# First conv chunk on unnormalised x: the tiles of chunk 0 take x times gain, and the row factor comes at their eviction

## The chip, the cores and the metric

The kernel runs on one core of a Trainium2 chip. The metric is the device time of one execution in microseconds; the engines named here are TensorE (PE, matmuls into the eight PSUM banks `ps`), VectorE (DVE), ScalarE (ACT), GpSimd (POOL, idle here) and SyncE (SP, which only issues transfers).

## What is computed

A block of 512 tokens of width 1024 in float32: a conv layer and an attention layer, each with a gated side input, and behind them a second block with its own attention, a recurrent branch and two feed-forward layers. The change lies in the first matmuls of the first layer:

```python
h = rms_norm(x, norm_g[0])              # x * rsqrt(mean(x*x) + EPS) * g, row by row (a row is a token)
u = h @ w_in
a, b, gate = jnp.split(u, [CONV_DIM, 2 * CONV_DIM], axis=-1)
y = a * jax.nn.sigmoid(b)
y = lax.conv_general_dilated(y, dw[:, None, :], window_strides=(1,), padding=((CONV_WIDTH - 1, 0),), ...,
                             feature_group_count=CONV_DIM) + dw_b      # 31 taps, each channel by itself
y = layer_norm(y, ln_g, ln_b)
y = jax.nn.silu(y) * jax.nn.silu(gate)
x = x + y @ w_out
```

The row factor rsqrt(mean(x*x) + EPS) is one number per token, so a matmul of x times gain can be multiplied by it afterwards.

## The kernel before

All activations lie with the channels on the 128 partitions and the 512 tokens along the free side; x is `X`, eight blocks of 128x512, loaded in four quarters of two blocks (128x1024). A matmul of full precision is made of three: each operand is cut into a high part (rounded to the matmul's input form) and a low part (the rest), and high times high, high times low and low times high are added in PSUM. So a weight tile of 128x1024 is first loaded into `w_raw` by SyncE, then ScalarE copies it to `w_hi`, and VectorE subtracts to `w_lo`; in the code of either engine this is `prep()`. There are four slots (`RING`): a load waits until the w_lo of the tile four before is done, and a w_hi until TensorE is through with it. TensorE's `tile()` is eight blocks of 128x128, three matmuls each, 24 in all.

Each engine has a program of its own, carried out in the order in which it is written, and they meet only at semaphores. Stage 0 is the conv layer's input, in eight chunks c of 128 channels. A chunk has four weight tiles: a, b, gate (all three on `H_hi`, `H_lo`, the normalised x), and a diagonal tile with eight of the 31 taps, on `cv_yh`, `cv_yl`, the halves of y = a * sigmoid(b). The other 23 taps are VectorE's (`cv_acc`), and its last addition gives `cv_Y` (`y_done`). TensorE adds up the columns of `cv_Y` of chunk c - 1 between the gate tile and the diagonal tile of chunk c, so it waits there for `y_done`, and then for `y_lo` of its own chunk. The tiles are numbered through: chunk 0 has tiles 0 to 3, chunk 1 has 4 to 7.

Ahead of chunk 0 stand the squares of x (ScalarE, `sq` and `tmp`), their sums by a matmul with ones into bank 7 (TensorE, `sq_used`), the guess of the row factor (`guess`, ScalarE, exp of -0.5 log), its Newton step (`newton`, VectorE, into `rx`), and `normed`: per block VectorE multiplies x, gain and factor into `tmp`, ScalarE copies it to `H_hi` and VectorE subtracts to `H_lo`. After these come two weight tiles' halves and `pl_hi`, `pl_lo`, the halves of the side input (`pl_raw`, 128x2048).

The transfers at the start: ScalarE's queue has parameters (128x364), constants (128x640) and the four quarters of x, SyncE's has four weight tiles, two loads of the side input and the late parameters, and then one weight tile after another.

## Time and profile before

| | |
|---|---|
| median of three runs | 2136.47 us (2135.02 to 2147.24) |
| the profiled execution | 2154.28 us |
| its span | 2152.5 us |
| TensorE busy in it | 2004.0 us (93%) |
| VectorE busy in it | 1237.8 us (58%) |
| ScalarE busy in it | 849.3 us (39%) |
| granted TensorE clock, mean over the span | 0.955 |

Times in the rows further down are microseconds from the span's start. Busy shares are means over stages of different kinds; for a change at the start, the rows of the start count.

### The profile page before, as it was taken

What the parts mean: (1) busy time and instruction counts of PE and PEld (TensorE: products, weight loads), DVE (VectorE), ACT (ScalarE), POOL (GpSimd) and SP (SyncE); (2) the same over time, 40 slices, a digit from 0 to 9 for tenths busy, and PEclk for the clock granted to TensorE, in tenths of its full rate; (3) what the DMA queues carried; (4) which work ended last, traced back from release to release, by engine and by line L of the source; (5) the groups of instructions that cost most, each with busy time, mean ns of one, the idle gap of its engine ahead of it and who ended that gap; (6) DMA issues with size and microseconds to landing.
All of it is one profiled execution on the core that took longest, in us unless ns stands there. A gap on an engine that the chain in (4) does not pass through costs nothing.

```text
span 2152.5 us, 23084 instructions
## 1 busy us (share of the span) xinstructions
PE 2004.0 (93%) x8460; PEld 1544.5 (72%) x8460; DVE 1237.8 (58%) x1859; ACT 849.3 (39%) x1156; POOL 0.2 (0%) x4
## 2 busy tenths in 40 slices
PE   6999788899999997899999989998898899999999
PEld 4888466677777676688888866666665578888887
DVE  5999666765766636644443355578654365444422
ACT  4333534344444334443432244444342334434311
POOL 0000000000000000000000000000000000000000
PEclk9999899899999879999999989989998999999999
DMA  4323222322212111233333412111211132332332
GB/s 169 100 78 100 91 69 69 103 74 64 63 53 64 42 49 59 77 99 97 91 103 114 132 59 89 49 39 49 69 59 39 46 110 90 97 97 93 103 116 89
DMA packets 49136, 175.17 MB, mean 81 GB/s; under 512 B 6048, under 2 KB 6176, under 8 KB 48288
## 3 DMA queue, kind: packets, MB, share of 16 engines
q1 hardware_dynamic: 44496, 159.67, 24.1%
q10 hardware_dynamic: 4560, 14.41, 2.0%
q8 instruction: 53, 0.87, 0.2%
q14 instruction: 27, 0.22, 0.0%
HBM read 166.19 MB, written 6.29 MB: 80 GB/s over the span
## 4 chain that ended last, share of the span: by engine, by line
PE 49%; DVE 8%; ACT 3%; issue 1%; DVEq 0%; ACTq 0%
PE ps L1471 45%; PE ps L1860 1%; DVE w_lo L904 1%; PE ps L1873 1%; DVE tmp L1325 1%; PE ps L1889 1%; ACT w_hi L418 1%; PE ps L1780 1%; DVE ds_acc L1245 1%; DVE ds_mx L1244 0%; DVE ds_P L1387 0%; DVE X L956 0%; DVE var L939 0%; DVE var L915 0%; DVE ds_P L1407 0%
## 5 line engine op out<-in xcount | busy, mean ns | idle before, releaser
L1471 PE MATMUL ps<-H_hi,w_hi 128*128 128x512 f32 x1600 | 658.3, 411 | 43.7 <-DVE H_lo L963 14.9
L1471 PE MATMUL ps<-H_lo,w_hi 128*128 128x512 f32 x1600 | 635.0, 397 | 0.0
L1471 PE MATMUL ps<-H_hi,w_lo 128*128 128x512 f32 x1600 | 633.9, 396 | 0.0
L904 DVE TENSOR_TENSOR w_lo<-w_raw,w_hi 128x1024 fp32r<-128x1024 f32 x298 | 363.2, 1223 | 368.6 <-ACT w_hi L418 363.9
L1471 PEld LDWEIGHTS ps<-H_hi,w_hi 128*128 128x128 f32 x1600 | 307.6, 192 | 141.4 <-issue 33.4
L418 ACT ACTIVATE w_hi<-w_raw 128x1024 fp32r<-128x1024 f32 x298 | 311.5, 1048 | 145.3 <-PE ps L1471 143.8
L1471 PEld LDWEIGHTS ps<-H_lo,w_hi 128*128 128x128 f32 x1600 | 308.3, 193 | 69.9 <-issue 8.6
L1471 PEld LDWEIGHTS ps<-H_hi,w_lo 128*128 128x128 f32 x1600 | 307.4, 192 | 66.5
L1471 PE MATMUL ps<-mid_hi,w_lo 128*128 128x512 f32 x352 | 138.8, 394 | 0.0
L1471 PE MATMUL ps<-mid_lo,w_hi 128*128 128x512 f32 x352 | 138.8, 394 | 0.0
L1471 PE MATMUL ps<-mid_hi,w_hi 128*128 128x512 f32 x352 | 138.8, 394 | 0.0
L1065 DVE SCALAR_TENSOR_TENSOR cv_acc<-cv_a,par,cv_acc 128x509 f32<-128x509 f32 (+6 forms) x168 | 111.4, 727 | 0.0
L418 ACT ACTIVATE mid_hi<-tmp 128x512 f32 x44 | 27.8, 632 | 195.4 <-DVE tmp L1029 195.4
L956 DVE SCALAR_TENSOR_TENSOR X<-ps,X 128x512 f32<-128x512 f32 (+1 forms) x36 | 27.0, 750 | 125.1 <-PE ps L1471 125.0
L466 ACT ACTIVATE r<-X 128x512 f32<-128x512 f32 x40 | 25.3, 632 | 175.6 <-DVE X L956 175.6
L1471 PE MATMUL ps<-G_hi,w_hi 128*128 128x512 f32 x128 | 54.6, 426 | 26.1 <-DVE X L956 10.5
L1471 PEld LDWEIGHTS ps<-mid_lo,w_hi 128*128 128x128 f32 x352 | 65.9, 187 | 16.3
L1471 PEld LDWEIGHTS ps<-mid_hi,w_hi 128*128 128x128 f32 x352 | 65.9, 187 | 16.2
L1471 PEld LDWEIGHTS ps<-mid_hi,w_lo 128*128 128x128 f32 x352 | 65.9, 187 | 16.1
L1025 DVE TENSOR_TENSOR tmp<-ps,rx 128x512 f32<-128x512 f32 x44 | 30.4, 691 | 68.1 <-PE ps L1471 68.1
L1496 PE MATMUL ps<-sq,con 128*128 128x512 f32 x84 | 50.0, 691 | 9.3 <-DVE rs L921 7.5
L521 ACT ACTIVATE sq<-sq 128x512 f32<-128x512 f32 x44 | 27.8, 633 | 77.2 <-DVE sq L1020 77.2
(295 smaller groups left out, 2421.0 us busy)
## 6 DMA issues: line engine op xcount, KB each, us to landing
w_raw<-weights SPq DMA_DIRECT2D x298, 512.0 KB, 3.6
X<-x ACTq DMA_DIRECT2D x4, 512.0 KB, 11.2
pl_P<-spill ACTq DMA_DIRECT2D x1, 2048.0 KB, 8.3
spill<-X ACTq DMA_DIRECT2D x8, 256.0 KB, 2.0
X<-spill ACTq DMA_DIRECT2D x2, 1024.0 KB, 5.1
out<-X SPq DMA_DIRECT2D x8, 256.0 KB, 5.1
at_mask<-masks ACTq DMA_DIRECT2D x1, 1536.0 KB, 6.2
at_pair<-at_raw ACTq DMA_DIRECT2D x96, 16.0 KB
```

Of the source, the lines that this page charges most:

```text
L418: return act.activation(out_ap, in_ap, ACT.Copy)
L466: act.activation(out_t, X[:, m:m + n, :], ACT.Square).then_inc(x_squared, 1)
L521: act.activation(sq[:, j, :], sq[:, j, :], ACT.Silu).then_inc(gated, 1)
L904: dve.tensor_tensor(w_lo[:, s, :], w_raw[:, s, :], w_hi[:, s, :].bitcast(F32), ALU.subtract)\
L956: dve.scalar_tensor_tensor(X[:, m:m + n, :], src, scale, X[:, m:m + n, :], ALU.mult, ALU.add)\
L1025: dve.tensor_tensor(tmp[:, j, :], ps[:, bank_of(k.n["prep"] - AHEAD - 1), :], rx[:, :], ALU.mult).then_inc(read_out, 1)
L1065: instr = dve.scalar_tensor_tensor(acc, a[:, 0:S - t], w, acc, ALU.mult, ALU.add)
L1245: link(dve.match_replace(acc, ds_mx[:, :], acc, TAKEN))
L1325: link(dve.reciprocal(tmp[:, 0, :], tmp[:, 0, :]))
L1471: mm = pe.matmul(ps[:, bank, :], w, x, start=first and n == 0 and q == 0, stop=last and n == len(blocks) - 1 and q == 2)
L1496: pe.matmul(ps[:, bank, :], ones if lhsT is None else lhsT, sq[:, (k.n[sq_done] - 1) % 2, :], start=c == 0, stop=c == n - 1).then_inc(sq_u ...
L1780: pe.matmul(ps[:, 6 + h % 2, 0:P * (b + 1)], ds_U[rows, 4 + h // 2, b * P:(b + 1) * P], ds_kvi[rows, 1, 0:P * (b + 1)], start=True, stop=T ...
```

## The change

The first conv chunk's three tiles run on `G_hi`, `G_lo`, the halves of x times gain without the row factor. ScalarE makes `G_hi` as each quarter lands, ahead of its square; VectorE makes `G_lo`. TensorE sums the squares inside tile 0, ahead of blocks 1, 3, 5 and 7. VectorE multiplies chunk 0's three results by the row factor `rx` when it takes them out of PSUM (`first_conv`, `first_gate`), and these evictions stand inside `normed`, behind its blocks 2 and 5. The other seven chunks still take `H_hi`, `H_lo`. SyncE's third transfer and all behind it wait for the second quarter of x. The weight tiles' halves move with it: the third tile's stand ahead of the guess, the fourth's in `first_conv`, the fifth's and sixth's in `first_gate`, and in chunk 0's taps there are two in place of four.

```diff
--- before.py
+++ after.py
@@ -22,6 +22,7 @@
 D = 1024
 KC = D // P
 RING = 4
+FIRST_CONV, FIRST_GATE = 2, 5
 AHEAD = 2
 EPS = 1e-6
 NEG = -1e30
@@ -374,6 +375,8 @@
         @block.sync
         def _(sp):
             for u in range(RING):
+                if u == 2:
+                    sp.wait_ge(x_loaded[1], 16)
                 sp.dma_start(w_raw[:, u, :], weights[u]).then_inc(landed[u], 16)
             for q in range(2):
                 sp.dma_start(pl_raw[:, 2 * q:2 * q + 2, :], ple_in[q]).then_inc(ple_loaded, 16)
@@ -532,26 +535,46 @@
                 act.dma_start(X[:, 2 * q:2 * q + 2, :], x_in[:, 2 * q:2 * q + 2, :]).then_inc(x_loaded[q], 16)
             begin(k, 0)
             prep()
+            act.wait_ge(par_loaded, 16)
             for q in range(4):
                 act.wait_ge(x_loaded[q], 16)
+                for m in (2 * q, 2 * q + 1):
+                    act.activation(G_hi[:, m, :], X[:, m, :], ACT.Copy, scale=col("norm_g0", m)).then_inc(split_hi, 1)
+                    k.up(split_hi)
                 if q >= 2:
                     act.wait_ge(sq_used, q - 1)
                 act.activation((sq, tmp)[q % 2][:, :, :], X[:, 2 * q:2 * q + 2, :], ACT.Square).then_inc(sq_done, 1)
                 k.up(sq_done)
                 if q == 1:
                     prep()
+            prep()
             logs()
-            act.wait_ge(par_loaded, 16)
             guess(7, 1.0 / D, sq_used, 4)
             for c in range(KC):
                 split(H_hi[:, c, :], c % 2)
-            prep()
-            prep()
+                if c == FIRST_CONV:
+                    act.wait_ge(scaled, k.up(scaled))
+                    act.activation(cv_sg[:, 0, :], cv_sg[:, 0, :], ACT.Sigmoid).then_inc(gated, 1)
+                    k.up(gated)
+                    act.wait_ge(read_out, k.up(read_out))
+                    copy(cv_yh[:, 0, PAD:PAD + S], cv_a[:, 0, :]).then_inc(y_hi, 1)
+                    k.up(y_hi)
+                    prep()
+                if c == FIRST_GATE:
+                    act.wait_ge(scaled, k.up(scaled))
+                    act.activation(cv_G[:, 0, :], cv_G[:, 0, :], ACT.Silu).then_inc(gate_out, 1)
+                    k.up(gate_out)
+                    prep()
+                    prep()
             act.wait_ge(ple_loaded, 32)
             copy(pl_hi[:, :, :], pl_raw[:, :, :]).then_inc(act_out, 1)
             k.up(act_out)
             k.up(dve_out)
-            for c in range(KC):
+            k.up(tile_done, 3 + DIAG[0])
+            prep()
+            for _ in range(DIAG[0]):
+                prep()
+            for c in range(1, KC):
                 act.wait_ge(tile_done, k.up(tile_done, 2))
                 if c >= 2:
                     act.wait_ge(read_out, k.at(read_out, -1))
@@ -963,7 +986,7 @@
                 dve.tensor_tensor(dst, src, hi.bitcast(F32), ALU.subtract).then_inc(split_lo, 1)
                 k.up(split_lo)
 
-            def normed(gain):
+            def normed(gain, between=()):
                 for c in range(KC + 1):
                     if c < KC:
                         if c >= 2:
@@ -973,6 +996,8 @@
                         k.up(tmp_done)
                     if c:
                         split(H_lo[:, c - 1, :], tmp[:, (c - 1) % 2, :], H_hi[:, c - 1, :])
+                    if c in between:
+                        between[c]()
 
             def ple(pl_P, hi, lo, gain):
                 prep()
@@ -1040,19 +1065,48 @@
             prep()
             prep()
             dve.wait_ge(par_loaded, 16)
+            for m in range(KC):
+                dve.wait_ge(split_hi, k.up(split_hi))
+                dve.scalar_tensor_tensor(G_lo[:, m, :], X[:, m, :], col("norm_g0", m), G_hi[:, m, :].bitcast(F32),
+                                         ALU.mult, ALU.subtract).then_inc(split_lo, 1)
+                k.up(split_lo)
+            prep()
             newton(7, 1.0 / D, rx, sq_used, 4)
-            normed("norm_g0")
-            prep()
-            prep()
+
+            def first_conv():
+
+                dve.wait_ge(tile_done, 2)
+                dve.tensor_tensor(cv_sg[:, 0, :], ps[:, 1, :], rx[:, :], ALU.mult).then_inc(scaled, 1)
+                k.up(scaled)
+                link(dve.tensor_tensor(cv_a[:, 0, :], ps[:, 0, :], rx[:, :], ALU.mult))
+                dve.wait_ge(gated, k.up(gated))
+                dve.tensor_tensor(cv_a[:, 0, :], cv_a[:, 0, :], cv_sg[:, 0, :], ALU.mult).then_inc(read_out, 1)
+                dve.wait_ge(read_out, k.up(read_out))
+                dve.wait_ge(y_hi, k.up(y_hi))
+                dve.tensor_tensor(cv_yl[:, 0, PAD:PAD + S], cv_a[:, 0, :], cv_yh[:, 0, PAD:PAD + S].bitcast(F32),
+                                  ALU.subtract).then_inc(y_lo, 1)
+                k.up(y_lo)
+                prep()
+
+            def first_gate():
+
+                dve.wait_ge(tile_done, 3)
+                dve.tensor_tensor(cv_G[:, 0, :], ps[:, 4, :], rx[:, :], ALU.mult).then_inc(scaled, 1)
+                k.up(scaled)
+                prep()
+                prep()
+
+            normed("norm_g0", between={FIRST_CONV + 1: first_conv, FIRST_GATE + 1: first_gate})
             dve.wait_ge(act_out, k.up(act_out))
             dve.tensor_tensor(pl_lo[:, :, :], pl_raw[:, :, :], pl_hi[:, :, :].bitcast(F32), ALU.subtract)\
                 .then_inc(dve_out, 1)
             k.up(dve_out)
             for c in range(KC):
-                dve.wait_ge(gated, k.up(gated))
                 a = cv_a[:, c % 2, :]
-                dve.tensor_tensor(a, ps[:, 2 * (c % 2), :], cv_sg[:, c % 2, :], ALU.mult).then_inc(read_out, 1)
-                dve.wait_ge(read_out, k.up(read_out))
+                if c:
+                    dve.wait_ge(gated, k.up(gated))
+                    dve.tensor_tensor(a, ps[:, 2 * (c % 2), :], cv_sg[:, c % 2, :], ALU.mult).then_inc(read_out, 1)
+                    dve.wait_ge(read_out, k.up(read_out))
                 for n, t in enumerate(DVE_TAPS[c]):
                     w = col("taps", 32 * c + CONV_W - 1 - t)
                     acc = cv_acc[:, n % 2, t:S]
@@ -1065,13 +1119,13 @@
                         instr = dve.scalar_tensor_tensor(acc, a[:, 0:S - t], w, acc, ALU.mult, ALU.add)
                     instr.then_inc(dve_chain, 1)
                     k.up(dve_chain)
-                    if n == 2:
+                    if n == 2 and c:
                         dve.wait_ge(y_hi, k.up(y_hi))
                         dve.tensor_tensor(cv_yl[:, c % 2, PAD:PAD + S], a, cv_yh[:, c % 2, PAD:PAD + S].bitcast(F32),
                                           ALU.subtract).then_inc(y_lo, 1)
                         k.up(y_lo)
                         prep()
-                    elif n in (5, 9, 13) or n == 14 and DIAG[c] == 2:
+                    elif n in ((5, 9, 13) if c else (9, 13)) or n == 14 and DIAG[c] == 2:
                         prep()
                 dve.wait_ge(dve_chain, k.at(dve_chain))
                 link(dve.tensor_tensor(cv_acc[:, 0, 1:S], cv_acc[:, 0, 1:S], cv_acc[:, 1, 1:S], ALU.add))
@@ -1454,7 +1508,7 @@
             k = Counts()
             k.up(x_summed)
 
-            def tile(groups, arriving=None, room=None):
+            def tile(groups, arriving=None, room=None, between=()):
 
                 s = k.n.get("tile", 0) % RING
                 k.up("tile")
@@ -1465,6 +1519,8 @@
                     for n, (b, x_hi, x_lo) in enumerate(blocks):
                         if arriving is not None:
                             pe.wait_ge(split_lo, arriving[n])
+                        if n in between:
+                            between[n](n // 2)
                         wh = w_hi[:, s, b * P:(b + 1) * P]
                         wl = w_lo[:, s, b * P:(b + 1) * P]
                         for q, (w, x) in enumerate(((wh, x_hi), (wh, x_lo), (wl, x_hi))):
@@ -1541,12 +1597,15 @@
 
             begin(k, 0)
             pe.wait_ge(con_loaded, 16)
-            for q in range(4):
+            def sums(q):
+
                 pe.wait_ge(sq_done, k.up(sq_done))
                 for j in range(2):
-                    mm = pe.matmul(ps[:, 7, :], ones, (sq, tmp)[q % 2][:, j, :], start=q + j == 0, stop=q + j == 4)
+                    mm = pe.matmul(ps[:, 7, :], ones, (sq, tmp)[q % 2][:, j, :], start=q + j == 0, stop=q + j == 4,
+                                   skip_group_check=True)
                 mm.then_inc(sq_used, 1)
                 k.up(sq_used)
+
             k.up(r0_done)
             k.up(rs_done)
             k.up(split_lo, KC)
@@ -1555,11 +1614,15 @@
                 if c >= 2:
                     pe.wait_ge(read_out, k.at(read_out, -1))
                 a = 2 * (c % 2)
-                tile([(a, True, True, blocks(H_hi, H_lo))], None if c else arrivals())
-                tile([(a + 1, True, True, blocks(H_hi, H_lo))])
+                if c == 1:
+                    k.up(split_lo, KC)
+                hi, lo = (H_hi, H_lo) if c else (G_hi, G_lo)
+                tile([(a, True, True, blocks(hi, lo))], arrivals() if c < 2 else None,
+                     between=() if c else {2 * q + 1: sums for q in range(4)})
+                tile([(a + 1, True, True, blocks(hi, lo))])
                 if c:
                     pe.wait_ge(gate_out, c)
-                tile([(4, True, True, blocks(H_hi, H_lo))])
+                tile([(4, True, True, blocks(hi, lo))])
                 if c:
                     pe.wait_ge(y_done, c)
                     pe.matmul(ps[:, 6, :], ones, cv_Y[:, c - 1, :], start=c == 1, stop=False, skip_group_check=True)
```

The two programs at three places, each engine's own order, with what an instruction waits for in brackets.

VectorE from its first weight halves on, before:

```order
L904 TENSOR_TENSOR w_lo<-w_raw,w_hi 128x1024 [waits hi_done] x2
L915 TENSOR_SCALAR var<-ps 128x512 [waits r0_done,par_loaded]
L919 TENSOR_TENSOR rx<-r 128x512 [waits dve_chain]
L920 SCALAR_TENSOR_TENSOR rx<-rx,var 128x512 [waits dve_chain]
L921 SCALAR_TENSOR_TENSOR rx<-rx,r 128x512 [waits dve_chain]
```

and now:

```order
L927 TENSOR_TENSOR w_lo<-w_raw,w_hi 128x1024 [waits hi_done] x2
L1070 SCALAR_TENSOR_TENSOR G_lo<-X,par,G_hi 128x512 [waits split_hi,par_loaded]
L1070 SCALAR_TENSOR_TENSOR G_lo<-X,par,G_hi 128x512 [waits split_hi] x7
L927 TENSOR_TENSOR w_lo<-w_raw,w_hi 128x1024 [waits hi_done]
L938 TENSOR_SCALAR var<-ps 128x512 [waits r0_done]
```

Eight G_lo have come between the second weight tile's low part and the Newton step, and the third tile's low part as well.

ScalarE from its first weight half to the guess, before (`r` is the guess's buffer):

```order
L418 ACTIVATE w_hi<-w_raw 128x1024 [waits landed0]
L539 ACTIVATE sq<-X 128x1024 [waits x_loaded0]
L539 ACTIVATE tmp<-X 128x1024 [waits x_loaded1]
L418 ACTIVATE w_hi<-w_raw 128x1024 [waits landed1]
L539 ACTIVATE sq<-X 128x1024 [waits sq_used,x_loaded2]
L539 ACTIVATE tmp<-X 128x1024 [waits sq_used,x_loaded3]
L441 ACT_TABLE_LOAD
L449 ACTIVATE r<-ps,par 128x512 [waits sq_used,par_loaded]
```

and now, up to the third square:

```order
L421 ACTIVATE w_hi<-w_raw 128x1024 [waits landed0]
L542 ACTIVATE G_hi<-X,par 128x512 [waits x_loaded0,par_loaded]
L542 ACTIVATE G_hi<-X,par 128x512
L546 ACTIVATE sq<-X 128x1024
L542 ACTIVATE G_hi<-X,par 128x512 [waits x_loaded1]
L542 ACTIVATE G_hi<-X,par 128x512
L546 ACTIVATE tmp<-X 128x1024
L421 ACTIVATE w_hi<-w_raw 128x1024 [waits landed1]
L542 ACTIVATE G_hi<-X,par 128x512 [waits x_loaded2]
L542 ACTIVATE G_hi<-X,par 128x512
L546 ACTIVATE sq<-X 128x1024 [waits sq_used]
```

The second weight tile's high part still stands behind the second square, which now has four G_hi ahead of it.

VectorE in the middle of the normalisation, where the first evictions are, now (before, the six rows with tmp and H_lo follow each other, and the product cv_a<-ps,cv_sg comes after all eight H_lo, two w_lo and pl_lo):

```order
L986 TENSOR_TENSOR H_lo<-tmp,H_hi 128x512 [waits split_hi]
L1079 TENSOR_TENSOR cv_sg<-ps,rx 128x512 [waits tile_done]
L1081 TENSOR_TENSOR cv_a<-ps,rx 128x512
L1083 TENSOR_TENSOR cv_a<-cv_a,cv_sg 128x512 [waits gated,dve_chain]
L1086 TENSOR_TENSOR cv_yl<-cv_a,cv_yh 128x512 [waits y_hi,read_out]
L927 TENSOR_TENSOR w_lo<-w_raw,w_hi 128x1024 [waits hi_done]
L994 SCALAR_TENSOR_TENSOR tmp<-X,par,rx 128x512 [waits split_lo]
L986 TENSOR_TENSOR H_lo<-tmp,H_hi 128x512 [waits split_hi]
```

Chunk 0's y and its halves have moved ahead of five of the eight H blocks; its taps stay behind pl_lo.

## Rows read from the trace of the kernel before

**Rows 1.** The page, busy time of each engine (share of the span) and its instructions

```profile
PE 2004.0 (93%) x8460; PEld 1544.5 (72%) x8460; DVE 1237.8 (58%) x1859; ACT 849.3 (39%) x1156; POOL 0.2 (0%) x4
```

**Rows 2.** Timeline of ScalarE, first 40 us: start, duration, instruction, idle before it

```profile
10.02 1.06 ACT L539 ACTIVATE sq<-X 128x1024 f32<-128x1024 f32 x1 [3.50 <-DMA X<-x]
12.58 1.06 ACT L539 ACTIVATE tmp<-X 128x1024 f32<-128x1024 f32 x1 [1.50 <-DMA X<-x]
13.54 1.04 ACT L418 ACTIVATE w_hi<-w_raw 128x1024 fp32r<-128x1024 f32 x1
...
21.14 0.69 ACT L449 ACTIVATE r<-ps,par 128x512 f32<-128x512 f32 x1 [1.08 <-PE ps L1547]
...
37.85 1.90 ACT L418 ACTIVATE pl_hi<-pl_raw 128x2048 fp32r<-128x2048 f32 x1
```

**Rows 3.** Timeline of TensorE: the sums, and where tiles 0, 1, 3, 4 and chunk 2 start

```profile
11.22 3.75 PE L1547 MATMUL ps<-sq,con 128*128 128x512 f32 x4 [11.22 <-ACT sq L539]
...
17.45 1.88 PE L1547 MATMUL ps<-sq,con 128*128 128x512 f32 x4
19.17 1.88 PE L1547 MATMUL ps<-tmp,con 128*128 128x512 f32 x4
27.80 0.77 PE L1471 MATMUL ps<-H_hi,w_hi 128*128 128x512 f32 x1 [6.75 <-DVE H_lo L963]
...
37.63 0.39 PE L1471 MATMUL ps<-H_hi,w_hi 128*128 128x512 f32 x1
...
48.52 0.40 PE L1471 MATMUL ps<-cv_yh,w_hi 128*128 128x512 f32 x1
...
54.11 0.39 PE L1471 MATMUL ps<-H_hi,w_hi 128*128 128x512 f32 x1
...
76.90 0.39 PE L1471 MATMUL ps<-H_hi,w_hi 128*128 128x512 f32 x1
```

**Rows 4.** Timeline of VectorE, up to chunk 2

```profile
14.62 1.23 DVE L904 TENSOR_TENSOR w_lo<-w_raw,w_hi 128x1024 fp32r<-128x1024 f32 x1 [6.83 <-ACT w_hi L418]
...
30.46 0.75 DVE L971 SCALAR_TENSOR_TENSOR tmp<-X,par,rx 128x512 f32<-128x512 f32 x1
...
39.78 2.29 DVE L1048 TENSOR_TENSOR pl_lo<-pl_raw,pl_hi 128x2048 fp32r<-128x2048 f32 x1 [0.39 <-ACT pl_hi L418]
...
44.64 0.55 DVE L1060 TENSOR_SCALAR cv_acc<-cv_a,par 128x512 f32<-128x512 f32 x1
...
65.00 0.69 DVE L1079 TENSOR_TENSOR cv_Y<-cv_acc,ps 128x512 f32<-128x512 f32 x1
65.84 0.69 DVE L1054 TENSOR_TENSOR cv_a<-ps,cv_sg 128x512 f32<-128x512 f32 x1 [0.16 <-ACT cv_sg L558]
...
68.09 0.68 DVE L1070 TENSOR_TENSOR cv_yl<-cv_a,cv_yh 128x512 fp32r<-128x512 f32 x1
...
88.66 0.69 DVE L1054 TENSOR_TENSOR cv_a<-ps,cv_sg 128x512 f32<-128x512 f32 x1 [1.05 <-ACT cv_sg L558]
```

**Rows 5.** Windows: from:to, length, each engine's busy time, granted clock, DMA share, GB/s

```profile
0.00:8.00 8.00, 0.00 (x0) 0.00 (x0) 1.41 (x3) 2.34 (x2) 0.20 (x4) 1.00 0.77 280
4.00:10.00 6.00, 0.00 (x0) 0.00 (x0) 1.23 (x1) 2.34 (x2) 0.00 (x0) 1.00 1.03 413
27.80:33.30 5.50, 5.50 (x12) 3.33 (x13) 5.36 (x9) 2.52 (x4) 0.00 (x0) 0.50 0.00 0
219.50:224.50 5.00, 0.02 (x1) 0.00 (x0) 4.90 (x8) 0.00 (x0) 0.00 (x0) 0.70 0.16 65
...
228.00:231.50 3.50, 3.45 (x4) 1.46 (x5) 3.50 (x6) 1.22 (x2) 0.00 (x0) 0.50 0.00 0
```

**Rows 6.** Timeline of ScalarE, two scaled copies and a weight half in a row

```profile
803.43 1.32 ACT L476 ACTIVATE G_hi<-X,par 128x512 fp32r<-128x512 f32 x2
804.66 1.04 ACT L418 ACTIVATE w_hi<-w_raw 128x1024 fp32r<-128x1024 f32 x1
```

## Prediction

> **What bounds the kernel now.** The page's busy line comes first: TensorE has work for 93% of the span, VectorE for 58% [rows 1]. Such an average hides the part that the diff touches, the first 77 us, so the timelines of the engines over that stretch come next. ScalarE squares each quarter of x when it lands, the first at 10.02 us and the second at 12.58, and takes the guess of the row factor once the sums of squares are there, at 21.14 [rows 2]. TensorE sums the squares from 11.22 to 21.05, is then idle for 6.75 us, runs the first tile from 27.80 to 37.63, and from there has tile after tile: tile 1 starts at 37.63, tile 3 at 48.52, tile 4 at 54.11, and the third chunk (chunk 2) begins at 76.90 [rows 3]. That last number is the yardstick of this forecast. From 76.90 to the end of the conv stage TensorE never stops: a chunk is four tiles and a column sum, VectorE has some 1 us to spare in each (its c=2 product waits 1.05 us for the sigmoid [rows 4]), and the product of chunk 1 has started at 65.84, 7 us before TensorE could use it. What the change makes of the time is what it makes of 76.90; everything behind it is moved with it.
>
> **TensorE alone gains.** The first conv chunk's three tiles now take x times gain, split (G_hi, G_lo), and the sums of squares are done between their blocks. So nothing on TensorE waits for the row factor until the diagonal tile. Its work is the same: 24 matmuls a tile and eight sums.
>
> **When x is there.** SyncE now holds its third and fourth weight tile, both ple loads and the late parameters until the second quarter of x has landed. Before, the transfers together moved 280 GB/s over the first 8 us, 2.24 MB, and 413 from 4 us on [rows 5]. Up to the first quarter there are now two weight tiles (0.52 MB each, 128x1024 of four bytes), parameters and constants (0.51, from 128x364 and 128x640) and the quarter itself (0.52), 2.08 MB, which is reached at 7.7 us; the second quarter follows 0.52 MB later, at 8.9. The two ends are 7.5 and, if nothing is won, the 10.0 of before. What speaks for 7.7 is the spacing of the quarters before [rows 2]: 2.56 us for 0.52 MB is 205 GB/s, half of what was moved. The Trainium skill says the same (DMA: Bandwidth & Descriptors, Issuing engines are not separate DMA queues): transfers of all issuing engines run on the same 16 DMA engines and interleave. By that rule the quarters come 1.3 us apart and the sum below holds; without it, it would be 2.3 us more.
>
> **What holds TensorE's start.** ScalarE does per quarter two scaled copies (1.23 us from start to the next start) and a square (0.96) [rows 2, 6]: 2.19 us. Two quarters from 7.7 end at 12.1, then comes the split of the second weight tile, to 13.15. VectorE's order is the point: its second w_lo stands ahead of all eight G_lo. It already waited 6.83 us for ScalarE's w_hi there, and everything behind it with it [rows 4]. So its second w_lo runs from 13.2 to 14.45, G_lo of block 0 to 15.2, and TensorE starts at 15.25, though x and the first G_hi were there at 8.4. The Trainium skill (TensorE: Matmul & The Clock Gate, Architectural detail) calls the queues of ScalarE and VectorE strictly first in, first out; by it this block stands in full, and without it the sum would be that of the second rival below.
>
> **When the sums are ready.** At 2.4 GHz a tile's 24 matmuls take 5.45 us (two of them 37.63 to 48.52), so a block of three 0.68, and two sums 1.72 (17.45 to 19.17); at 1.2 GHz I take 1.28 for a block and 3.4 for two sums, near twice that, as the first two of before bear out (3.75 with their end) [rows 3]. The clock rose after some 5.7 us of work both times that it starts from rest here (from 27.80 it was 0.50 up to 33.3 at least, and the second pair of sums, between 11.22 and 17.45, is the last that is slow) [rows 3, 5]. From 15.25: block 0 to 16.5, first sums to 19.95, block 1 to 21.1 with the clock rising at about 20.95, block 2 to 21.8, sums 23.5, two blocks 24.9, sums 26.6, two blocks 28.0, last sums 29.85. ScalarE keeps ahead of that (its third square may start at 19.95, its fourth at 23.5). Before, the sums ended at 21.05. **The row factor comes 8.8 us later**, since the 24 matmuls are now in its way and start late. TensorE itself ends the first tile at 30.4 and the third at 41.3, 7.2 us before the 48.52 of before.
>
> **VectorE's chain, from 29.85.** Guess, Newton steps and the first three H splits follow as before (VectorE is through with the third block at 30.46) [rows 4], all 8.8 later: 39.25. Then comes what is new. Two evictions with the row factor and the product, 0.73 each (a VectorE pass over 128x512 is 0.69 [rows 4], 0.04 for the wait on it): 41.45. ScalarE's sigmoid (0.6) lies under the second of them. The copy to cv_yh with its hand-over 0.75, the split 0.7: 42.9. The fourth weight tile's halves follow one after the other and end at 44.4, where the diagonal tile can start: TensorE has waited 3.15 us. Three pairs of a product and a split, 1.39 each (two passes, as eight before): 48.6. Eviction of the gate: 49.3; ScalarE's silu to 50.0, then its weight split, then VectorE's: 52.25, where tile 4 starts (TensorE free at 50.05: 2.2 of idle). The next w_lo to 53.4, the last H splits to 55.5. Now VectorE waits for pl_hi, which ScalarE can only begin after the last H_hi: 54.8 plus 1.90, and pl_lo takes 2.29: 59.05 [rows 2, 4]. Then the taps of chunk 0: from 44.64 to 65.69 it was 21.05 us [rows 4]; a split (0.68) and two w_lo (1.23 each) have gone elsewhere, less the 0.1 that each lies over the next: 18.2. **Chunk 0's y ends at 77.25, where it ended at 65.69.** Within it the w_lo for the gate tile of chunk 1, now behind ten taps (0.66 each after two shorter ones, 6.1), ends at 66.35; TensorE, free at 63.15, waits 3.2 and is through at 71.8.
>
> **The place where it is paid.** TensorE waits for that y before the column sum (y_done), 5.5 us, and then for y_lo of chunk 1, which takes 2.93 after the product may start (65.84 to 68.77 [rows 4]): 80.2. The diagonal tile (5.59, as 48.52 to 54.11) ends at 85.85, against 76.90: **+8.95 us**. From there TensorE is the bound again: VectorE is up to 1.8 us late in chunk 2 and regains 1 a chunk.
>
> **The clock after the 5.5 us.** Before, after an idle stretch of 5.00 us that ended at 224.5 the granted clock was 0.50 until 231.5, 7 us past the restart, and after 6.75 us idle it stayed low for some 6 more [rows 3, 5]. With the restart at 77.3 the diagonal tile from 80.25 runs at 1.2 GHz up to 83.3 or 84.3 and loses 1.5 to 2.0 us; I take 1.8. The ends are 0, if the clock holds, and 5.6, if it is low for the whole tile. The earlier waits (3.15, 2.2, 3.2) may cost clock too, but VectorE is what is waited for up to 77.3 and covers it. The extra work that nobody waits for (SyncE's held loads: the third weight tile lands near 13, is split by ScalarE at about 25 and needed at 35.9; ple near 17, needed at 54.8) I put at nothing: their cover is 10 us and more.
>
> **Sum.** 8.95 + 1.8 = +10.8 us. The profiled execution took 2154.28 us (2152.5 of span and 1.8 around it), so one of the changed kernel should take 2165; the median of the runs is 2136.47, 17.8 lower, over the same stages, and with the same addition gives **2147.3**.
>
> **Rivals.**
> - *TensorE's gain stays.* If VectorE were in time, the 7.2 us of the third tile would be kept: 2129.3. For it: TensorE has 93% of the span, VectorE 58%, and 6.75 us before were its idle wait for the row factor. Against it: VectorE was busy without a break from 44.64 to 65.69 and has got 8 passes for G_lo, 3 evictions and several handshakes; chunk 2 at 69.7 wants the diagonal tile at 64.1 and so y of chunk 0 by 61. It is the case on the other side. 12%.
> - *G_lo isn't held behind the second w_lo.* TensorE would start at 9.2, the sums end at 23.7 (then bound by ScalarE's squares), the chain would be 6.1 shorter: 85.85 becomes 79.8, +2.9, so 2139.4. Against it: the order of VectorE's program and the 6.83 us of before. 8%.
> - *Holding the loads brings nothing.* x at 10.0: +2.3 more, 2149.6. 12%.
> - *The clock stays low through the diagonal tile*, because four waits in 36 us make it fall again and again: 8.95 + 5.6, 2151.0. 8%.
>
> **How the numbers follow.** My forecast has 60%. The single runs of before lie 12 us apart, so even its exact case can be read 2 or 3 us off. The range 2135 to 2153 takes in the forecast with its ends and all rivals but the gain. A difference of 1% is 21 us, about what a measurement of this kernel can tell from none; no case reaches it: 1% for faster, 97% within, 2% for slower (the last two rivals together and one more wait of the kind).
>
> **What would show it.** In the profile of the changed kernel: the first scaled copy starts near 7.7; VectorE's second w_lo ends at 14.4 with G_lo right behind; the last sum of squares ends near 29.9; the diagonal tile starts near 44.4 after a wait for VectorE; y of chunk 0 at 77.3; TensorE idle for over 5 us ahead of the first column sum; chunk 2 begins at 86 to 88. The prediction is wrong if TensorE starts before 12, if the sums end before 26, or if chunk 2 begins before 77.

## The result and the profile after

| | before | changed |
|---|---|---|
| median of 17 runs each | 2135.21 us | 2151.34 us |
| lowest to highest | 2133.65 to 2152.28 | 2145.09 to 2166.35 |
| ratio, with 95% interval | | 1.0055 [1.0028, 1.0081] |
| the profiled execution, its span | 2154.28, 2152.5 | 2157.8, 2155.7 |
| granted clock in it | 0.955 | 0.961 |
| chunk 2 starts | 76.90 [rows 3] | 86.89 |
| last y of the conv stage ends | 224.47 | 234.43 |

The changed kernel is slower by 0.55% by the ratio, which is 11.7 us of 2135.21, with an interval of 6 to 17 us; the two medians lie 16.1 us apart. The forecast was 10.8 us. The yardstick of the forecast, the start of chunk 2, has moved by 9.99 us, and 150 us later the shift is still 9.96: nothing is won back within the conv stage.

The page's busy line of the changed kernel is nearly that of [rows 1], and tells nothing of this:

```profile
PE 1996.6 (93%) x8460; PEld 1539.1 (71%) x8460; DVE 1244.2 (58%) x1870; ACT 854.3 (40%) x1164; POOL 0.2 (0%) x4
```

ScalarE's timeline of the changed kernel, against [rows 2]:

```profile
8.56 1.33 ACT L542 ACTIVATE G_hi<-X,par 128x512 fp32r<-128x512 f32 x2 [2.27 <-DMA X<-x]
9.79 1.04 ACT L546 ACTIVATE sq<-X 128x1024 f32<-128x1024 f32 x1
...
20.25 1.06 ACT L546 ACTIVATE sq<-X 128x1024 f32<-128x1024 f32 x1 [5.07 <-PE ps L1604]
...
29.59 0.69 ACT L452 ACTIVATE r<-ps,par 128x512 f32<-128x512 f32 x1 [2.92 <-PE ps L1604]
```

The first quarter of x is there 1.46 us sooner than before, and the third square now waits 5.07 us for TensorE, whose sums stand inside the first tile. The guess, 21.14 before, comes at 29.59. VectorE's timeline, against [rows 4]:

```profile
13.98 1.22 DVE L927 TENSOR_TENSOR w_lo<-w_raw,w_hi 128x1024 fp32r<-128x1024 f32 x1 [6.44 <-ACT w_hi L421]
15.12 4.06 DVE L1070 SCALAR_TENSOR_TENSOR G_lo<-X,par,G_hi 128x512 fp32r<-128x512 f32 x6
...
38.72 0.68 DVE L1079 TENSOR_TENSOR cv_sg<-ps,rx 128x512 f32<-128x512 f32 x1
...
55.54 2.29 DVE L1101 TENSOR_TENSOR pl_lo<-pl_raw,pl_hi 128x2048 fp32r<-128x2048 f32 x1 [1.11 <-ACT pl_hi L421]
...
75.23 0.69 DVE L1133 TENSOR_TENSOR cv_Y<-cv_acc,ps 128x512 f32<-128x512 f32 x1
...
78.07 0.68 DVE L1124 TENSOR_TENSOR cv_yl<-cv_a,cv_yh 128x512 fp32r<-128x512 f32 x1
```

Six G_lo start in one piece right behind the second w_lo, ahead of which VectorE stood idle for 6.44 us: their inputs had become ready one after the other since 9. The chain from the guess on then ends at 75.92, where it ended at 65.69. TensorE's timeline, against [rows 3]:

```profile
16.02 0.76 PE L1527 MATMUL ps<-G_hi,w_hi 128*128 128x512 f32 x1 [16.02 <-DVE G_lo L1070]
...
17.43 2.78 PE L1604 MATMUL ps<-sq,con 128*128 128x512 f32 x4
...
21.45 1.88 PE L1604 MATMUL ps<-tmp,con 128*128 128x512 f32 x4
...
27.67 1.88 PE L1604 MATMUL ps<-tmp,con 128*128 128x512 f32 x4
...
43.87 0.47 PE L1527 MATMUL ps<-cv_yh,w_hi 128*128 128x512 f32 x1 [2.42 <-DVE w_lo L927]
...
51.30 0.50 PE L1527 MATMUL ps<-H_hi,w_hi 128*128 128x512 f32 x1 [1.59 <-DVE w_lo L927]
...
65.19 0.47 PE L1527 MATMUL ps<-H_hi,w_hi 128*128 128x512 f32 x1 [2.74 <-DVE w_lo L927]
...
75.97 2.07 PE L1628 MATMUL ps<-cv_Y,con 128*128 128x512 f32 x2 [5.09 <-DVE cv_Y L1133]
...
78.80 0.80 PE L1527 MATMUL ps<-cv_yh,w_hi 128*128 128x512 f32 x1 [0.76 <-DVE cv_yl L1124]
...
86.89 0.39 PE L1527 MATMUL ps<-H_hi,w_hi 128*128 128x512 f32 x1
```

The one idle stretch of 6.75 us ahead of tile 0 has become five later ones, all for VectorE: 2.42, 1.59, 2.74, 5.09 and 0.76 us. The fourth is the one that decides: the column sum waits 5.09 us for chunk 0's y. Windows over that place, with the columns of [rows 5] (the five busy times are of TensorE, its weight loads, VectorE, ScalarE and GpSimd):

```profile
65.00:70.00 5.00, 4.81 (x21) 4.05 (x22) 5.00 (x9) 0.00 (x0) 0.00 (x0) 1.00 0.34 111
70.00:75.00 5.00, 0.88 (x4) 0.38 (x3) 4.97 (x9) 0.00 (x0) 0.00 (x0) 0.89 0.29 98
75.00:80.00 5.00, 3.27 (x5) 1.50 (x6) 4.93 (x9) 3.43 (x5) 0.00 (x0) 0.50 0.00 0
80.00:85.00 5.00, 5.00 (x15) 3.89 (x14) 5.00 (x8) 0.98 (x2) 0.00 (x0) 0.59 0.49 144
```

VectorE is busy for all but 0.1 us from 65 to 85, TensorE works 0.88 us of the five from 70, and the granted clock falls with it and is back only in the course of the fourth window: the diagonal tile takes 8.09 us (78.80 to 86.89), where chunk 0's took 5.59 in [rows 3] and chunk 1's own 5.99 in the kernel before (70.91 to 76.90).

### The profile page after: what moved, and what is told of

Read it like the earlier page. It is cut to its first block, busy times and chain, and to the rows that moved or that the text cites. A ratio compares the mean times of both kernels' runs of the same rounds, so it can differ in the third digit from the quotient of the medians.

```text
span 2155.7 us, 23107 instructions
## 1 busy us (share of the span) xinstructions
PE 1996.6 (93%) x8460; PEld 1539.1 (71%) x8460; DVE 1244.2 (58%) x1870; ACT 854.3 (40%) x1164; POOL 0.2 (0%) x4
## 4 chain that ended last, share of the span: by engine, by line
PE 49%; DVE 9%; ACT 3%; issue 1%; DVEq 0%; ACTq 0%
PE ps L1527 44%; PE ps L1923 1%; DVE w_lo L927 1%; PE ps L1936 1%; PE ps L1952 1%; DVE tmp L1379 1%; DVE ds_acc L1299 1%; PE ps L1843 1%; ACT w_hi L421 1%; DVE ds_mx L1298 1%; DVE ds_P L1441 0%; DVE X L979 0%; DVE var L962 0%; DVE var L938 0%; DVE rs L944 0%
## 5 line engine op out<-in xcount | busy, mean ns | idle before, releaser
L1527 PE MATMUL ps<-H_hi,w_hi 128*128 128x512 f32 x1576 | 642.5, 408 | 40.7 <-DVE H_lo L974 11.7
L1527 PE MATMUL ps<-H_lo,w_hi 128*128 128x512 f32 x1576 | 621.0, 394 | 0.0
L1527 PE MATMUL ps<-H_hi,w_lo 128*128 128x512 f32 x1576 | 620.2, 394 | 0.0
L1527 PEld LDWEIGHTS ps<-H_hi,w_hi 128*128 128x128 f32 x1576 | 300.3, 191 | 133.8 <-issue 28.0
L1527 PEld LDWEIGHTS ps<-H_lo,w_hi 128*128 128x128 f32 x1576 | 300.7, 191 | 68.1 <-issue 8.3
L1527 PEld LDWEIGHTS ps<-H_hi,w_lo 128*128 128x128 f32 x1576 | 300.1, 190 | 64.5
L1527 PE MATMUL ps<-G_hi,w_hi 128*128 128x512 f32 x152 | 65.6, 432 | 41.4 <-DVE G_lo L1070 16.0
L1527 PEld LDWEIGHTS ps<-G_hi,w_hi 128*128 128x128 f32 x152 | 29.4, 193 | 54.8 <-issue 34.0
L1527 PE MATMUL ps<-G_lo,w_hi 128*128 128x512 f32 x152 | 61.6, 405 | 0.0
```

The source lines that it names most:

```text
L1527: mm = pe.matmul(ps[:, bank, :], w, x, start=first and n == 0 and q == 0, stop=last and n == len(blocks) - 1 and q == 2)
```

## Experiments

All starts and ends below are in us from the span's start. None of the eight kernels leaves anything out. Early_half, sums_ahead, filler and before_hold ran beside each other on one chip (before: median 2136.7 of 31 runs), the other four on another (before: 2140.8 of 32); the ratio of the changed kernel is that of the section above. Repeats of one kernel spread over 12 to 26 us, so the question of what a step costs is answered by one profile of each kernel, at the start of chunk 2, and the ratio tells whether the whole time follows. Of the ratios, those of the changed kernel, no_hold, filler and early_half lie clear of 1 above it and second_bank's below it; no two of the changed kernel's variants up to pl_early can be told apart by them.

| | last sums end | y of chunk 0 ends | from the one to the other | chunk 2 starts | last y ends | ratio to before |
|---|---|---|---|---|---|---|
| before | 21.05 | 65.69 | 44.64 | 76.90 | 224.47 | 1 |
| changed | 29.55 | 75.92 | 46.37 | 86.89 | 234.43 | 1.0055 [1.0028, 1.0081] |
| before_hold | 19.96 | 64.62 | 44.66 | 75.84 | 223.41 | 0.9984 [0.9948, 1.0020] |
| no_hold | 31.39 | 77.77 | 46.38 | 88.66 | 236.23 | 1.0063 [1.0032, 1.0095] |
| early_half | 24.49 | 70.86 | 46.37 | 82.08 | 229.62 | 1.0039 [1.0002, 1.0075] |
| filler | 31.00 | 77.38 | 46.38 | 85.96 | 233.53 | 1.0066 [1.0028, 1.0104] |
| sums_ahead | 20.78 | 69.24 | 48.46 | 80.33 | 227.86 | 1.0024 [0.9990, 1.0058] |
| pl_early | 30.79 | 73.76 | 42.97 | 83.81 | 231.38 | 1.0024 [0.9995, 1.0053] |
| reordered | 21.04 | 64.48 | 43.44 | 74.97 | 222.51 | 1.0001 [0.9971, 1.0032] |
| second_bank | 20.99 | 65.62 | 44.63 | 68.54 | 222.23 | 0.9949 [0.9917, 0.9981] |

The fourth column is the table's point: in four kernels whose sums end between 24.49 and 31.39 it is the same within 0.01 us. As long as VectorE's order behind the sums is kept and TensorE is in time, whatever moves the sums moves y by as much. Where the sums come at 20.78 (sums_ahead), TensorE isn't in time any more.

### The weight half that holds VectorE (early_half)

The theory is that ScalarE's second weight half, late behind two quarters' work, holds VectorE's whole queue. It goes ahead of x, and nothing else changes:

```diff
             prep()
+            prep()
             act.wait_ge(par_loaded, 16)
             for q in range(4):
                 act.wait_ge(x_loaded[q], 16)
...
-                if q == 1:
-                    prep()
```

> The changed kernel with one step moved: ScalarE makes the second weight tile's high part right after the first, ahead of x, so that VectorE's second w_lo no longer stands in front of G_lo. Theory A (VectorE's chain behind the row factor sets chunk 2, and the blocked G_lo is a part of its lateness): TensorE starts near 10.1 us in place of 16.02, the last sums end near 24.7 in place of 29.6, and chunk 2 begins 4.9 us earlier than the changed kernel's 86.89, at 82.0, so still 5 us behind the 76.90 of before. Rival B (the block costs nothing, since TensorE's three tiles have room): chunk 2 stays at 86.9. The whole time should follow by as much, under what the repeats differ by.

VectorE and TensorE of that kernel:

```profile
8.19 1.23 DVE L926 TENSOR_TENSOR w_lo<-w_raw,w_hi 128x1024 fp32r<-128x1024 f32 x1 [0.70 <-ACT w_hi L421]
9.50 0.75 DVE L1069 SCALAR_TENSOR_TENSOR G_lo<-X,par,G_hi 128x512 fp32r<-128x512 f32 x1
```

```profile
10.39 0.76 PE L1526 MATMUL ps<-G_hi,w_hi 128*128 128x512 f32 x1 [10.39 <-DVE G_lo L1069]
...
22.61 1.88 PE L1603 MATMUL ps<-tmp,con 128*128 128x512 f32 x4
...
82.08 0.39 PE L1526 MATMUL ps<-H_hi,w_hi 128*128 128x512 f32 x1
```

The wait ahead of w_lo has shrunk from 6.44 to 0.70 us, TensorE starts 5.63 us sooner, the sums end 5.06 sooner, and chunk 2 starts at 82.08, 4.81 us sooner, where 82.0 was expected. So half of what the change costs hung on the place of one ScalarE copy. The first G_hi starts at 8.56 in the changed kernel and at 8.65 here, so G_lo's input is there at about 9.3 in both; the first G_lo starts at 15.12 in the one and at 9.50 in the other. It was only its place in the queue that held it. The Trainium skill (TensorE: Matmul & The Clock Gate, Architectural detail) calls ScalarE's and VectorE's queues strictly first in, first out, and the trace agrees.

### The sums ahead of the tile (sums_ahead)

```diff
+            for q in range(4):
+                sums(q)
...
-                     between=() if c else {2 * q + 1: sums for q in range(4)})
+                     between=())
```

> The changed kernel with the sums of squares back ahead of tile 0; the tiles still take x times gain without the row factor. Theory A (the sums inside tile 0 delay the row factor, and with it VectorE's chain): the last sums end near 20.7 in place of 29.6; VectorE then waits for tile 1, so the chain gains 6.8 us, and chunk 2 begins near 80.1, 3 us behind before. Rival B (TensorE's order doesn't matter, only its total): tile 2 ends 4 us earlier or later and chunk 2 moves by under 2 us. Rival C (what costs is the added evictions on VectorE alone): chunk 2 stays within 1 us of 86.9.

TensorE:

```profile
18.90 1.88 PE L1604 MATMUL ps<-tmp,con 128*128 128x512 f32 x4
...
20.22 0.80 PE L1527 MATMUL ps<-G_hi,w_hi 128*128 128x512 f32 x1
...
80.33 0.39 PE L1527 MATMUL ps<-H_hi,w_hi 128*128 128x512 f32 x1
```

The sums end at 20.78, 8.77 us sooner than in the changed kernel, and chunk 2 starts 6.56 us sooner, at 80.33 (80.1 was expected). Most of the difference is 2.09 us in the chain, and its row shows why: VectorE is free for the first eviction at 30.04 and waits for tile 1.

```profile
32.02 0.69 DVE L1079 TENSOR_TENSOR cv_sg<-ps,rx 128x512 f32<-128x512 f32 x1 [1.98 <-PE ps L1527]
```

This is the largest single step of the loss. The steps don't add up, since this one and early_half both work through the end of the sums (6.56 and 4.81 us are more than the 9.99 of the loss together). It also shows what the reordering can do at best: TensorE is then what the chain waits for. Yet chunk 2 is still 3.43 us later than before. The early sums alone don't mend it.

### The clock after the wait (filler)

Five matmuls whose result nobody reads, into bank 7 (free by then), stand ahead of the wait for y of chunk 0:

```diff
                 tile([(4, True, True, blocks(hi, lo))])
+                if c == 1:
+                    for j in range(5):
+                        pe.matmul(ps[:, 7, :], ones, X[:, j, :], start=True, stop=True, skip_group_check=True)
                 if c:
                     pe.wait_ge(y_done, c)
```

> The changed kernel with five extra float32 matmuls (x with ones, into bank 7, read by nobody) on TensorE ahead of its wait for chunk 0's y; they take 4.3 us of the 5.1 that it idles there. Theory A (the clock falls in that idle stretch, and the diagonal tile of chunk 1 pays for it): the granted clock stays at 1.00 from 70 to 90 us, the diagonal tile takes 5.6 us in place of 8.1, and chunk 2 begins near 84.4 in place of 86.9. Rival B (the idle stretch costs nothing beyond itself): chunk 2 stays at 86.9 or comes later by what the filler overlaps.

TensorE, and two of its windows:

```profile
17.57 3.61 PE L1604 MATMUL ps<-sq,con 128*128 128x512 f32 x4
...
73.74 4.45 PE L1628 MATMUL ps<-X,con 128*128 128x512 f32 x10
...
80.27 0.50 PE L1527 MATMUL ps<-cv_yh,w_hi 128*128 128x512 f32 x1 [1.22 <-DVE cv_yl L1124]
...
85.96 0.39 PE L1527 MATMUL ps<-H_hi,w_hi 128*128 128x512 f32 x1
```

```profile
75.00:80.00 5.00, 4.05 (x10) 1.52 (x8) 4.89 (x9) 1.97 (x3) 0.00 (x0) 1.00 0.00 0
80.00:85.00 5.00, 4.73 (x20) 3.88 (x21) 5.00 (x7) 2.44 (x3) 0.00 (x0) 1.00 0.38 108
```

The granted clock stays at 1.00, where it was 0.50 and 0.59, and the diagonal tile takes 5.69 us in place of 8.09. That is 2.4 us for the clock. One profile alone would be thin evidence, since the clock had its own course in this execution (it was also low from 66.5 to 69.9, in the gate tile, so that without the five matmuls TensorE would have idled 3.5 us here and not 5.1). But the six kernels that wait 4.65 to 5.10 us at this place all run the tile behind it at the low clock for a part, in 7.16 to 8.33 us (pl_early 7.16, reordered 7.59, no_hold 8.00, changed 8.09, sums_ahead 8.20, early_half 8.33). Chunk 2 starts only 0.93 us sooner (85.96, where 84.4 was expected), since in this execution the sums came 1.45 us later: the first pair took 3.61 us and not 2.78, with the same instructions ahead of it. That part is no effect of the edit. The ratio of 1.0066 is not below the change's 1.0055, and the intervals overlap widely, so a gain in the whole time was not measured.

### The held loads (before_hold, no_hold)

The wait on SyncE alone, in the kernel before, and the change without it:

```diff
@@ before_hold, against before
+                if u == 2:
+                    sp.wait_ge(x_loaded[1], 16)
@@ no_hold, against the changed kernel
-                if u == 2:
-                    sp.wait_ge(x_loaded[1], 16)
```

> The kernel before with one line of the change: SyncE's third and later loads wait for the second quarter of x; nothing else is changed. If the hold is what brings x early and the row factor's chain is what bounds the start, the first square starts near 8.6 in place of 10.02, the sums end 2 to 2.5 us earlier than 21.05, and chunk 2 begins at 74.4 to 75 in place of 76.90: a gain of 2 us, which the timing of whole runs can't tell. Rival: the sums run at the lower clock whatever x does, and the chain gains under 1 us.

> The changed kernel without SyncE's wait for the second quarter of x: all loads are issued at once, as before. If the hold is what brings x early (the kernel before with the hold alone had its first square at 8.61 in place of 10.02), the first scaled copy starts near 10.0 in place of 8.56, VectorE's blocked G_lo moves with it, and chunk 2 begins 1.4 us later than the changed kernel's 86.89, at 88.3. Rival (the hold is hidden behind ScalarE's own work): chunk 2 stays at 86.9.

ScalarE and TensorE of before_hold, and the first G_hi of no_hold:

```profile
8.61 1.06 ACT L541 ACTIVATE sq<-X 128x1024 f32<-128x1024 f32 x1 [2.19 <-DMA X<-x]
...
13.67 1.06 ACT L541 ACTIVATE sq<-X 128x1024 f32<-128x1024 f32 x1 [1.77 <-PE ps L1549]
```

```profile
9.81 3.75 PE L1549 MATMUL ps<-sq,con 128*128 128x512 f32 x4 [9.81 <-ACT sq L541]
...
13.36 3.17 PE L1549 MATMUL ps<-tmp,con 128*128 128x512 f32 x4
...
75.84 0.39 PE L1473 MATMUL ps<-H_hi,w_hi 128*128 128x512 f32 x1
```

```profile
10.22 1.33 ACT L540 ACTIVATE G_hi<-X,par 128x512 fp32r<-128x512 f32 x2 [3.78 <-DMA X<-x]
```

The hold brings the first quarter of x from 10.02 to 8.61 in the one kernel and from 10.22 to 8.56 in the other. Without it the change is 1.77 us later at chunk 2 (1.4 was expected). In the kernel before it is worth only 1.06 of its 1.41 us. There the first sums run at about half the rate, 3.75 and 3.17 us for a pair where later pairs take 1.88, whatever the time at which x comes, and the third square waits 1.77 us for them. (The granted clock reads 1.00 over both the slow and the fast pairs there, so the rate has to be taken from the passes themselves.) The larger gain that I expected there, 1.9 to 2.5 us, was wrong, and the smaller one of the rival, under 1 us, was nearer. The Trainium skill (DMA: Bandwidth & Descriptors, Issuing engines are not separate DMA queues) says that transfers of all issuing engines run on the same 16 DMA engines and interleave; the 1.66 us by which one queue's wait advances another's transfer agree.

### The side input's halves (pl_early)

ScalarE's pl_hi goes ahead of the guess, VectorE's pl_lo ahead of the Newton step, off the chain:

```diff
@@ ScalarE, behind the third prep() (VectorE likewise, ahead of newton; the old places are empty)
+            act.wait_ge(ple_loaded, 32)
+            copy(pl_hi[:, :, :], pl_raw[:, :, :]).then_inc(act_out, 1)
```

> The changed kernel with the side input's halves (pl_hi on ScalarE, pl_lo on VectorE) moved ahead of the guess, where both engines are idle in its profile (from 26.6 to 31). Theory A (VectorE's chain from the row factor to y of chunk 0 is what TensorE waits for): the chain loses pl_lo and its wait for pl_hi, 3.3 us, y of chunk 0 ends at 72.6 in place of 75.92, TensorE's 2.7 us of idle ahead of the gate tile go, and chunk 2 begins at 83.6, or near 81.2 if the idle stretch, now 4.6 us, doesn't let the clock fall. Rival (TensorE's own order bounds it): chunk 2 stays within 1 us of 86.9.

VectorE:

```profile
28.45 2.29 DVE L1075 TENSOR_TENSOR pl_lo<-pl_raw,pl_hi 128x2048 fp32r<-128x2048 f32 x1 [0.58 <-ACT pl_hi L421]
...
73.07 0.69 DVE L1133 TENSOR_TENSOR cv_Y<-cv_acc,ps 128x512 f32<-128x512 f32 x1
```

The chain is 3.40 us shorter, which is pl_lo's 2.29 and its wait of 1.11, to the hundredth. Chunk 2 comes 3.08 us sooner, although the sums came 1.24 us later in this execution (again by the first pair, 3.62 us): 2.16 us is what the chain less that delay gives, and the rest is the diagonal tile, 7.16 us in place of 8.09. With 1.24 us added, the 83.6 that was expected would have been 84.8; it came at 83.81.

### Both reorderings, and y ahead of the taps (reordered, second_bank)

"reordered" takes the sums ahead as sums_ahead does, makes the side input's halves early but at other places than pl_early (pl_hi right behind the guess, pl_lo ahead of the first evictions), and moves ScalarE's silu of chunk 0 behind the last H_hi:

```diff
@@ ScalarE, the silu; the edits of the sums and of the side input's halves aren't shown
             for c in range(KC):
                 split(H_hi[:, c, :], c % 2)
...
                 if c == FIRST_GATE:
-                    act.wait_ge(scaled, k.up(scaled))
-                    act.activation(cv_G[:, 0, :], cv_G[:, 0, :], ACT.Silu).then_inc(gate_out, 1)
-                    k.up(gate_out)
                     prep()
                     prep()
...
+            act.wait_ge(scaled, k.up(scaled))
+            act.activation(cv_G[:, 0, :], cv_G[:, 0, :], ACT.Silu).then_inc(gate_out, 1)
+            k.up(gate_out)
```

> The changed kernel with three moves: sums of squares ahead of tile 0 (measured alone: chunk 2 at 80.33), the side input's halves early (ScalarE right behind the guess, VectorE ahead of the first evictions, where it waits for tile 1), and ScalarE's silu of chunk 0 behind the two weight halves that VectorE waits 1.65 us for. By the chain: y of chunk 0 ends at 69.24 - 3.3 - 1.6 + 0.3 = 64.6, and chunk 2 begins at 73.1 with the clock up, 75.6 with it down, 1.3 to 3.8 us ahead of the kernel before. If something else than VectorE's chain bounds it, chunk 2 stays above 78.

TensorE:

```profile
64.54 1.93 PE L1629 MATMUL ps<-cv_Y,con 128*128 128x512 f32 x2 [4.66 <-DVE cv_Y L1132]
...
74.97 0.39 PE L1526 MATMUL ps<-H_hi,w_hi 128*128 128x512 f32 x1
```

The y of chunk 0 ends at 64.48 (64.6 was expected), chunk 2 starts at 74.97 (75.6 with the clock down), 1.93 us ahead of the kernel before, and the ratio is 1.0001. So with three things in another order the change costs nothing. Whether the tiles on unnormalised x have a part in the 1.93 us isn't shown: the held loads alone gave 1.06 of it in the kernel before, and no run puts the side input's halves early there. It gains nothing worth speaking of either, since TensorE still waits 4.66 us for VectorE's taps and runs the next tile at the low clock (7.59 us).

"second_bank" attacks that wait: VectorE makes chunk 1's product and its low half within chunk 0's taps, and the diagonal tile of chunk 1 goes to bank 7, ahead of the column sum, so that TensorE has 24 matmuls to do while y is unfinished:

```diff
@@ VectorE, in the taps of chunk 0 (beside the edits of reordered)
+                    if n == 13 and c == 0:
+                        prep()
+                        dve.wait_ge(gated, k.up(gated))
+                        dve.tensor_tensor(cv_a[:, 1, :], ps[:, 2, :], cv_sg[:, 1, :], ALU.mult).then_inc(read_out, 1)
...
@@ TensorE
-                if c:
+                def columns():
...
+                if c > 1:
+                    columns()
...
-                    tile([(5, d == 0, d == DIAG[c] - 1, ...
+                    tile([(7 if c == 1 else 5, d == 0, d == DIAG[c] - 1, ...
+                if c == 1:
+                    columns()
```

> As the run before it, and the wait for y of chunk 0 is taken from TensorE's way: chunk 1's product and split stand among chunk 0's last taps on VectorE, its diagonal tile has a bank of its own (7) and comes ahead of the column sum. If that wait (5.1 us) and the clock that falls in it are what keeps the unnormalised tiles from paying, TensorE has no idle stretch over 3 us before chunk 2, which begins near 67, 10 us ahead of the kernel before. VectorE then is the bound of the conv stage with 21.9 us a chunk: its last y ends near 218 in place of 224.5, and the fastest run lies 6 us under the fastest of before. Rival: the gain ends at chunk 2 and TensorE gives all of it back, the last y at 221 or later.

TensorE:

```profile
59.79 0.50 PE L1541 MATMUL ps<-cv_yh,w_hi 128*128 128x512 f32 x1
...
65.68 1.13 PE L1644 MATMUL ps<-cv_Y,con 128*128 128x512 f32 x2
...
68.54 0.47 PE L1541 MATMUL ps<-H_hi,w_hi 128*128 128x512 f32 x1 [1.74 <-DVE w_lo L927]
...
86.16 1.13 PE L1644 MATMUL ps<-cv_Y,con 128*128 128x512 f32 x2 [1.02 <-DVE cv_Y L1147]
...
89.00 0.79 PE L1541 MATMUL ps<-cv_yh,w_hi 128*128 128x512 f32 x1 [1.72 <-DVE cv_yl L1138]
```

Chunk 2 starts at 68.54 (67 was expected), 8.36 us ahead of before. Then comes the wait that was moved and not removed: 1.02 us for y of chunk 1 at 86.16, 1.72 us for y_lo at 89.00, and the clock falls from 88.3 to 95.1. At the last y 2.24 us of the lead are left, which is what the rival had (221 or later; 222.23 came), not the 218 that I expected. I had taken VectorE's 21.9 us a chunk for the bound; after chunk 2 it is TensorE's 22.8, as the prediction itself had read from the trace of before. It is still the one kernel whose ratio lies clear of 1 on the fast side: 0.9949 [0.9917, 0.9981], 10.9 us less by the ratio and 6.7 by the medians; its lowest run is 2.4 us below the lowest of before, where 6 was expected. Only 2.24 us of that stand in the conv stage. And "reordered", whose last y ends just 0.28 us later and whose program is the same from there on, has a ratio of 1.0001. So the second bank's own worth in the finished kernel is 0.28 us as far as the profiles show, and the rest of the 0.5% isn't shown to be its effect.

## Why the prediction was right

The forecast (0.50% slower, 2147.3 us, range 2135 to 2153) has come out: 0.55%, median 2151.34, and the steps of the mechanism came in their order: G_lo held, the sums late, VectorE's chain, the wait for y, the clock. That the ratio's 11.7 us lie so near the 10.8 is in part luck, since the repeats come in clusters (last section) and the medians give 16.1. The median is also what the last rival gave (2151.0), but its mechanism didn't happen: the diagonal tile lost 2.4 us to the clock and not 5.6.

- **When x is there**: 7.7 was said, 8.56 measured, late by 0.86. The bytes moved before x aren't the whole of it; the end that the text gave for an unused hold, 10.0, is what no_hold shows (10.22).
- **What holds TensorE's start**: the second w_lo at 13.98 to 15.20 (13.2 to 14.45 was said), TensorE at 16.02 (15.25). early_half shows the cause: without that block it starts 5.63 us sooner.
- **When the sums are ready**: 29.55 against 29.85. Two errors cancel here. The start was 0.77 us late, and the clock's rise came sooner than the 5.7 us of work that the trace of before had shown twice: it was put near the end of block 1, and the passes speed up inside the first pair, which took 2.22 us up to the next start (17.43 to 19.65) and not the 3.4 of the text. With its end the pair took 2.78 us here, 2.63 in no_hold, 3.34 in early_half, 3.61 in filler and 3.62 in pl_early, so that term can't be had closer than a microsecond from one trace.
- **VectorE's chain**: 47.40 us from the sums to y of chunk 0 was the sum of the text, 46.37 came. The pieces: to the first eviction 9.17 (9.40 said), to the diagonal tile 5.15 (5.15), to tile 4 7.43 (7.85), to the end of pl_lo 6.53 (6.80), the taps 18.09 (18.20). Passes were counted with a hand-over each where some of these lay over each other. pl_early and sums_ahead test two of its links: taking out pl_lo shortens it by exactly its row, and bringing the factor earlier pays until tile 1 is in the way.
- **The place where it is paid**: the idle ahead of the column sum is 5.09 us (5.5 said), y_lo ends at 78.75 (80.2).
- **The clock after the 5.5 us**: the one term that was mis-sized by a third. 1.8 us was said, within ends of 0 and 5.6; the tile took 8.09 us against 5.69 with the clock up in filler, which makes 2.4.
- **Sum**: chunk 2 at 87.65 by the text with the clock in it, 86.89 measured: 1.40 us off for the earlier chain, 0.64 on for the longer diagonal tile. The step "everything behind it is moved with it" held through the conv stage (9.96 at the last y). One reading beside the sum was off: the product of chunk 1 starts 5.1 us before TensorE takes its y (65.84 to 70.91), not 7; no term used it.

The rivals: TensorE's gain did not stay, since all of it went into waits for VectorE; G_lo was held, and the price put on that rival, +2.9 us at chunk 2 if it weren't, left out the clock (early_half stands at +5.18, with a tile of 8.33 us); the hold brought 1.66 us of its 2.3; the clock was low for most of the diagonal tile but not all of it. The profiled execution, put at 2165, took 2157.8, and its span is only 3.2 us over that of before. Followed from one VectorE instruction to its like, the shift is 9.96 at 234 us, about 6.4 at 723, 0.2 at 1624 and 3.2 from 1710 on. It changes in stages whose program is the same in both; what the clock does there is the last section's matter. It need not change: in filler's profile the shift against before is 9.06 at the last y, 8.8 at 300 us and 8.8 at the end, and its span is 8.8 us over that of before. Which of the two spans is the odd one, two profiles can't say, and the 95% interval of the ratio, 6 to 17 us, holds the forecast.

## What to carry to other kernels

Work that is taken off the path of the engine that is 93% busy is worth nothing if the result it needs later comes by a chain of another engine: follow the chain from the last input to the first place where the busy engine waits for it, and check what was put in front (here 24 matmuls in front of a sum, and a late weight half at the head of a queue in front of eight passes that were ready). An extra wait of some 5 us on TensorE also cost clock in the next tile, 2.4 us here, so at chunk 2 filling that stretch with real work (another bank and another order, 8.36 us ahead of before) was worth more than shortening it (1.93). But a lead gained at the start lasts only as far as the engine that bounds the rest of the stage lets it: 150 us on the two stood 2.24 and 1.96 us ahead.

## What the hardware did that was not expected

Repeats of one kernel come in clusters 5 to 20 us apart. The changed kernel's 17 runs lie at 2145 to 2148 (8 of them), at 2151, at 2158 (3) and at 2163 to 2166 (5). Two profiles show one place where such a difference arises. Kernels before and before_hold have the same program behind the start, and the second is 1.07 us ahead at 236 us, 2.1 at 717 and 8.3 at 776. The windows of before, then of before_hold:

```profile
755.00:760.00 5.00, 5.00 (x24) 3.92 (x22) 1.92 (x6) 1.11 (x3) 0.00 (x0) 0.50 0.01 5
760.00:765.00 5.00, 5.00 (x20) 3.69 (x21) 1.12 (x3) 1.69 (x3) 0.00 (x0) 0.50 0.00 0
```

```profile
755.00:760.00 5.00, 5.00 (x33) 4.30 (x31) 1.80 (x6) 1.84 (x3) 0.00 (x0) 0.84 0.01 3
760.00:765.00 5.00, 5.00 (x35) 4.11 (x33) 2.25 (x8) 2.40 (x4) 0.00 (x0) 1.00 0.00 0
```

TensorE is busy in both, but the granted clock is 0.50 (1.2 GHz) from 743.7 to 777.9 in the one and from 743.0 to 756.6 in the other, with an idle stretch of 3.92 us in both (to 745.93 and to 743.45). Over the whole span it is low for 196 us against 146, and the span is 19.9 us longer with 1.06 us of that from the start. So with the same instructions a fall of the clock can cost 6 us more or less, and a shift of a few microseconds at the start is seen in the whole time only over many runs. Whether the phase of the start decides which it will be, or chance, isn't settled. The lowest run of each kernel, less the lowest of before in its session, follows the shift at the last y, in brackets: +11.4 for the changed kernel (+9.96), +8.8 for filler (+9.06), +6.5 for early_half (+5.15), +3.3 for sums_ahead (+3.39), -1.9 for before_hold (-1.06), -1.1 for reordered (-1.96), -2.4 for second_bank (-2.24), with pl_early (+9.3 against +6.91) and no_hold (+15.7 against +11.76) the worst fits.
